# The down product of a SwiGLU layer in the seven-product form, over even and odd chunks

## The chip, the cores and the metric

One core of one Trainium2 chip runs the whole program in one launch. The metric is the device time in microseconds (us) of one execution; before the change it is 2521.99 us (median of 3 runs, 2521.57 to 2523.63).

## The reference, cut to what matters

One layer of a streaming encoder over 560 tokens (16 meta, 512 prompt, 32 sample). All data is fp32, D_MODEL = 2048, D_FF = 5632.

```python
xn = rms_norm(h, g_pre_mix); proj = xn @ w_in           # 2048 x 6144
attn = stick-breaking attention, 8 heads; conv = gated short conv, 8 groups
h = h + rms_norm(mix @ w_out, g_post_mix)               # 2048 x 2048
xf = rms_norm(h, g_pre_ffn)
ff = silu(xf @ w_gate) * (xf @ w_up)                    # 2048 x 5632, twice
h = h + rms_norm(ff @ w_down, g_post_ffn)               # 5632 x 2048
```

The feed-forward part needs only the 544 tokens after the meta tokens (TL = 544, in two halves of TH = 272).

## The kernel before

Activations lie transposed: a chunk is 128 features on the partitions, tokens in the free dimension. Every matmul takes a 128x128 block of weights and 272 (or 280) tokens. Each fp32 product is made of three fp32r matmuls: rounded weights times rounded activations, rounded weights times the rest of the activations, rest of the weights times rounded activations. So every tile of weights (128 x 1024 values) is read by a DMA, rounded by ScalarE (`copy` into `t_hi`) and its rest taken by VectorE (`tile_rest`, `tensor_tensor` subtract into `t_lo`). Both live in a ring of RING_T = 4 tiles; ScalarE may round tile i only when the product of tile i - 4 is done (`tile_high`, L1313).

The stages in order of time: input transposed and normalised; heads and conv groups (loops over pairs, partly `Fori` hardware loops on each engine); out product; norm; gate and up products; down product; last norm, transposes and stores.

**Gate and up.** They use a seven-product form of a 2x2 block product (Strassen-Winograd): the 16 input chunks are split into halves A11..A22 (chunk halves 0 to 7 and 8 to 15, by token halves), and each step (44 of them; even ones gate, odd ones up) makes two output chunks from two panels of weights (8 chunks x 256 columns, 1 MB each). Seven tiles B11, B21, T2, T3, T1, T4, B22 (T1 to T4 are combinations that VectorE makes with `combine`, L1708) give seven products of 8 x 3 = 24 matmuls (`product`, L955). The combinations of the activations, `xs`, are made once. Products accumulate in three PSUM banks of a step in the order "acababa"; what is needed from a bank in between is copied out by ScalarE (`m1`, `u2`, `m7`) or added by VectorE (`c11`, `c22`, `c21`). The last product of a step, B22, waits for `c22_made` (the wait stands ahead of `product` for q == B22).

**SwiGLU.** In each even step VectorE multiplies the pair's values into `hid` (2 chunks x 544), ScalarE rounds them (`round_hidden`, L1352), VectorE takes the rest (`hidden_rest`, L1786), and SyncE stores both to DRAM (L573, L574).

**Down.** The plain form: 44 chunks of hidden values times 16 output chunks, in 4 blocks of 12, 12, 12 and 8 chunks. For each block and each pair of output chunks a tile of 4 chunks x 256 columns (`down_raw`, 6 buffers, L595) is loaded, split and multiplied with both token halves of the block's hidden values (`ffs`, loaded from DRAM for a whole block, L600): 48 matmuls per tile (L1004). The sums stay in PSUM over a block, then VectorE copies or adds 128 x 544 values to `y` (L1851, L1855). The hidden values of the next-but-one block are loaded when a block has ended. In the last block ScalarE squares finished chunks, GpSimd adds the squares, and two pairs of matmuls (L716) sum them over partitions for the last norm.

**Queues.** All loads and stores named here are issued by SyncE (SP) in one written order, each behind its waits, and are served in turn. Each other engine too runs its instructions in the order written.

Of the kernel before, what the change touches and what calls it, by code (L numbers as in the profile page):

```python
# [20 lines left out]
F32 = mybir.dt.float32  # L21
# [8 lines left out]
def build_layer(nc, x_prompt, x_sample, cache_k, cache_v, state_conv, meta, w_in, w_out, conv_w,  # L30
# [85 lines left out]
    with ExitStack() as ctx:  # L116
# [34 lines left out]
        def carve(at, n):  # L151
# [34 lines left out]
        gate = sb_at("gate", 189440, [P, 2, TL])  # L186
        hid = sb_at("hid", 193792, [P, 2, TL])
        hid_hi = sb_at("hid_hi", 198144, [P, 2, TL], F32R)
        hid_lo = sb_at("hid_lo", 202496, [P, 2, TL], F32R)
        ffs = sb_at("ffs", 0, [P, 2, max(SUBS), 2, SUB, TL], F32R)  # L190
        down_raw = [sb_at(f"down_raw{j}", at + h * 4096, [P, SUB, 2 * P])
                    for j, (at, h) in enumerate((at, h) for at in (181248, 121856, 173056) for h in range(2))]
        y_parts = [sb_at("y_left", 104448, [P, KH, TL]), sb_at("y_right", 189440, [P, KH, TL])]
        h2_back = sb_at("h2_back", 0, [P, KC, TL])
        y_tok = sb_at("y_tok", 34816, [P, 4, QB + 1, P])
        y_sq = [sb_at(f"y_sq{j}", 45056 + j * TL * 4, [P, TL]) for j in range(2)]
        y_sq_sum = sb_at("y_sq_sum", 45056 + 2 * TL * 4, [P, TL])
# [4 lines left out]
        ff_hi_scr = nc.dram_tensor("ff_hi_scr", (P, FF, TL), F32, kind="Internal").ap()  # L202
        ff_lo_scr = nc.dram_tensor("ff_lo_scr", (P, FF, TL), F32, kind="Internal").ap()
# [133 lines left out]
        hid_made = sem("hid_made")  # L337
        hid_rounded = sem("hid_rounded")
# [3 lines left out]
        down_loaded = [sem(f"down_loaded{j}") for j in range(6)]  # L342
        ffs_loaded = [[sem(f"ffs_loaded{j}_{k}") for k in range(3)] for j in range(2)]
        down_left = sem("down_left")
# [88 lines left out]
        w_down_v = w_down[0].rearrange("(k p) n -> p k n", p=P)  # L433
# [3 lines left out]
        DOWN0 = 7 * STEPS  # L437

        down_tiles = [(b, m, u) for b in range(len(SUBS)) for m in range(KC // 2) for u in range(SUBS[b])]
        first_chunk = [SUB * sum(SUBS[:b]) for b in range(len(SUBS))]  # L440
        first_tile = [KC // 2 * sum(SUBS[:b]) for b in range(len(SUBS))]

# [9 lines left out]

        def block_of_weights(step, half, n):
            return panel_of(step, half)[0][:, :, n * P:(n + 1) * P]

        def raw_tile(i):

            step, q = i // 7, i % 7
            if q == T2:
                return t2_raw[:, :, :]  # L460
            half, n = {B11: (0, 0), T1: (0, 0), T3: (0, 1), B21: (1, 0), T4: (1, 0), B22: (1, 1)}[q]
            return block_of_weights(step, half, n)

        def tile_of(ring, i):
            return ring[:, i % RING_T, :].rearrange("p (k n) -> p k n", n=P)
# [4 lines left out]
        def quarter(buf, t, n):  # L470
            return buf[:, n, t * TH:(t + 1) * TH]

        def down_tile_of(ring, i):
            return ring[:, i % RING_T, :].rearrange("p (k n) -> p k n", n=2 * P)
# [5 lines left out]
        def _(sp):  # L480
# [53 lines left out]
            with sp.Fori(0, HEADS // 2 - 1) as r:  # L534
                load_pair(r + 1, HEAD_COLS)
            with sp.Fori(HEADS // 2, (HEADS + GROUPS) // 2) as p:
                load_pair(p, CONV_COLS)
# [16 lines left out]
            with sp.Fori(2, KC // 2) as q:  # L554
                load_out(q)

            def load_panel(step, half):
                tile, loaded, _ = panel_of(step, half)
                src = gate_up[step % 2][:, KH * half:KH * (half + 1), step // 2 * 2 * P:(step // 2 + 1) * 2 * P]
                sp.dma_start(tile[:, :, :], src).then_inc(loaded, 16)  # L560
# [10 lines left out]
            def store_hidden(j):  # L571
                sp.wait_ge(hid_split, j + 1)
                sp.dma_start(ff_hi_scr[:, 2 * j:2 * j + 2, :], hid_hi[:, :, :].bitcast(F32)).then_inc(hid_stored, 16)  # L573
                sp.dma_start(ff_lo_scr[:, 2 * j:2 * j + 2, :], hid_lo[:, :, :].bitcast(F32)).then_inc(hid_stored, 16)  # L574

            for step in range(1, STEPS):
# [6 lines left out]
                if step > 3 and step % 2 == 0:  # L583
                    store_hidden(step // 2 - 2)
                load_panel(step, 0)
# [17 lines left out]
            for d in range(6):
                if d % 2 == 0:
                    sp.wait_ge(tile_lo, (7 * (LAST - 1) + 7, 7 * LAST + T1 + 1, 7 * LAST + 7)[d // 2])
                load_down(d)
                if d % 2:
                    continue
                sp.wait_ge(product_done, 7 * LAST + d // 2 + 1)
                if d == 0:  # L610
                    sp.wait_ge(hid_stored, 32 * (FF // 2 - 1))
                load_hidden(0, d // 2)
            for u in range(3):
                sp.wait_ge(product_done, 7 * LAST + 4 + u)
                load_hidden(1, u)
            store_hidden(FF // 2 - 1)
            for d in range(6, len(down_tiles)):
                b, m, u = down_tiles[d]
                if m == 1 and u == 0 and b in (1, 2):
                    sp.wait_ge(product_done, DOWN0 + first_tile[b])  # L620
                    sp.wait_ge(hid_stored, 32 * (FF // 2))
                    for v in range(SUBS[b + 1]):
                        load_hidden(b + 1, v)
                if m == 1 and u == 0 and b == 3:
                    sp.wait_ge(product_done, DOWN0 + first_tile[b])
                    sp.dma_start(h2_back[:, :, :], h_scr[:, :, LATE]).then_inc(h2_back_loaded, 16)
                sp.wait_ge(tile_lo, DOWN0 + d - 6 + 1)
                load_down(d)
# [15 lines left out]
        def _(pe):  # L644
# [245 lines left out]
            with pe.Fori(1, HEADS // 2) as p:  # L890
# [4 lines left out]
            with pe.Fori(HEADS // 2 + 1, (HEADS + GROUPS) // 2) as p:  # L895
# [35 lines left out]
            with pe.Fori(1, KC // 2) as q:  # L931
# [52 lines left out]
            for d, (b, m, u) in enumerate(down_tiles):  # L984
                i = DOWN0 + d
                pair = b * KC // 2 + m
                pe.wait_ge(tile_lo, i + 1)
                if m == 0:
# [991 lines left out]
```

## Time and profile before

| | us |
|---|---|
| median of 3 runs | 2521.99 |
| the profiled execution | 2524.61 |
| its span, first to last instruction | 2522.9 |
| TensorE matmul busy (18716 matmuls) | 2440.0 (97%) |
| VectorE busy | 1252.4 (50%) |
| ScalarE busy | 915.5 (36%) |
| granted TensorE clock, mean | 0.981 |

The page's chain of work that ended last lies 90% on TensorE: 36% on L955 (gate and up), 30% on L422 (input and out products), 19% on L1004 (down). A matmul's listed duration (about 290 ns) overlaps its neighbours'; the distance between two is what counts.

### The profile page before, as it was taken

Reading aid. Unit: us, or ns where it says so; the run is one execution under the profiler, and the core shown is the slowest. Engines: PE = TensorE matmul, PEld = TensorE weight load, DVE = VectorE, ACT = ScalarE, POOL = GpSimd, SP = SyncE. Lnnn points to the kernel's source line nnn. Section 1 sums busy time; section 2 is a strip of 40 time slices with the busy share of each in tenths; the row PEclk is TensorE's granted clock in tenths of the full one; section 3 lists DMA queues with packets and bytes.
Section 4 is the critical chain, followed back from the end, with each engine's and each line's share of the span. In section 5 each row is a group of like instructions: output and inputs, shape, how many; then the busy total and the mean of one; then the engine's idle time right before and its main releaser. Section 6 shows DMA issues by size and latency. Waiting matters only on the chain.

```text
span 2522.9 us, 43292 instructions
## 1 busy us (share of the span) xinstructions
PE 2440.0 (97%) x18716; PEld 2394.1 (95%) x18716; DVE 1252.4 (50%) x1387; ACT 915.5 (36%) x1177; POOL 99.0 (4%) x155
## 2 busy tenths in 40 slices
PE   8999999999999985999999999999999999999997
PEld 7999999999999984999999999999999999999996
DVE  5324332444353228777777767676765222222144
ACT  6344444422342224444444444444443111111123
POOL 0000000000011100000000000000000000000024
PEclk9999999999999996999999999999999999999997
DMA  7223222232225321434343434333336516242222
GB/s 235 83 64 89 80 80 65 85 92 84 80 70 167 89 75 64 134 119 136 118 137 118 137 118 136 119 131 124 126 129 262 187 43 232 76 171 85 105 93 71
DMA packets 313049, 290.66 MB, mean 115 GB/s; under 512 B 8348, under 2 KB 296500, under 8 KB 309956
## 3 DMA queue, kind: packets, MB, share of 16 engines
q1 hardware_dynamic: 298528, 281.70, 34.5%
q10 hardware_dynamic: 14372, 6.77, 0.9%
q8 instruction: 118, 1.93, 0.3%
q14 instruction: 31, 0.25, 0.0%
HBM read 245.82 MB, written 42.61 MB: 114 GB/s over the span
## 4 chain that ended last, share of the span: by engine, by line
PE 90%; DVE 5%; DMA 2%; ACT 2%; SPq 1%; issue 1%; POOL 0%; POOLq 0%; ACTq 0%; DVEq 0%
PE ps L955 36%; PE ps L422 30%; PE ps L1004 19%; PE ps L722 4%; DMA down_raw<-in_w_down_dram 2%; DVE xs L1716 1%; PE ps L666 1%; DMA misc<-in_x_sample_dram 0%; DVE misc L1720 0%; DVE y_left L1880 0%; DVE wide L1685 0%; DVE misc L1689 0%; DVE y_right L1880 0%; ACT xs L1320 0%; DVE t_lo L1695 0%
## 5 line engine op out<-in xcount | busy, mean ns | idle before, releaser
L955 PE MATMUL ps<-xs,t_hi 128*128 128x272 f32 x4928 | 940.5, 291 | 33.1 <-DVE xs L1716 19.1
L955 PEld LDWEIGHTS ps<-xs,t_hi 128*128 128x128 f32 x4928 | 780.9, 190 | 34.7 <-issue 32.2
L955 PE MATMUL ps<-xs,t_lo 128*128 128x272 f32 x2464 | 716.6, 291 | 0.0
L1004 PE MATMUL ps<-ffs,t_hi 128*128 128x272 f32 x2816 | 470.7, 290 | 12.7 <-DVE y_right L1855 7.3
L955 PEld LDWEIGHTS ps<-xs,t_lo 128*128 128x128 f32 x2464 | 467.3, 190 | 0.0
L1695 DVE TENSOR_TENSOR t_lo<-panel,t_hi 128x1024 fp32r<-128x1024 f32 x261 | 319.4, 1224 | 255.7 <-ACT t_hi L1313 255.7
L422 PE MATMUL ps<-act_hi,w_hi 128*128 128x272 f32 (+1 forms) x2048 | 435.4, 294 | 3.5 <-DVE act_lo L1532 2.3
L422 PE MATMUL ps<-act_lo,w_hi 128*128 128x272 f32 (+1 forms) x2048 | 427.0, 290 | 0.0
L422 PE MATMUL ps<-act_hi,w_lo 128*128 128x272 f32 (+1 forms) x2048 | 426.8, 290 | 0.0
L1004 PEld LDWEIGHTS ps<-ffs,t_hi 128*128 128x128 f32 x2816 | 402.2, 190 | 13.4 <-issue 7.5
L1313 ACT CAST t_hi<-panel 128x1024 fp32r<-128x1024 f32 x261 | 272.8, 1045 | 191.8 <-PE ps L955 185.4
L422 PEld LDWEIGHTS ps<-act_hi,w_hi 128*128 128x128 f32 x2048 | 322.8, 189 | 7.5 <-DVE act_lo L1532 3.0
L422 PEld LDWEIGHTS ps<-act_hi,w_lo 128*128 128x128 f32 x2048 | 324.2, 189 | 0.0
L422 PEld LDWEIGHTS ps<-act_lo,w_hi 128*128 128x128 f32 x2048 | 323.8, 189 | 0.0
L1004 PE MATMUL ps<-ffs,t_lo 128*128 128x272 f32 x1408 | 293.3, 290 | 0.0
L1791 DVE TENSOR_TENSOR t_lo<-down_raw,t_hi 128x1024 fp32r<-128x1024 f32 x88 | 109.8, 1248 | 304.1 <-ACT t_hi L1358 304.1
L408 DVE TENSOR_TENSOR w_lo<-w_raw,w_hi 128x1024 fp32r<-128x1024 f32 x126 | 157.9, 1254 | 192.2 <-ACT w_hi L402 190.7
L1358 ACT CAST t_hi<-down_raw 128x1024 fp32r<-128x1024 f32 x88 | 92.2, 1048 | 403.2 <-PE ps L1004 305.8
L402 ACT CAST w_hi<-w_raw 128x1024 fp32r<-128x1024 f32 x128 | 133.7, 1046 | 282.8 <-PE ps L422 222.1
L1004 PEld LDWEIGHTS ps<-ffs,t_lo 128*128 128x128 f32 x1408 | 221.7, 190 | 0.0
L1346 ACT ACTIVATE m<-ps 128x272 f32<-128x272 f32 x88 | 34.9, 397 | 150.1 <-PE ps L955 150.1
L1313 ACT CAST t_hi<-t_raw 128x1024 fp32r<-128x1024 f32 x44 | 46.2, 1049 | 69.3 <-PE ps L955 69.3
(174 smaller groups left out, 1547.1 us busy)
## 6 DMA issues: line engine op xcount, KB each, us to landing
w_raw<-in_w_in_dram SPq DMA_DIRECT2D x96, 512.0 KB, 3.8
panel<-in_w_up_dram SPq DMA_DIRECT2D x44, 1024.0 KB, 5.1
down_raw<-in_w_down_dram SPq DMA_DIRECT2D x88, 512.0 KB, 5.2
panel<-in_w_gate_dram SPq DMA_DIRECT2D x43, 1024.0 KB, 6.4
w_raw<-in_w_out_dram SPq DMA_DIRECT2D x32, 512.0 KB, 3.9
ff_hi_scr<-hid_hi SPq DMA_DIRECT2D x22, 544.0 KB, 2.7
ff_lo_scr<-hid_lo SPq DMA_DIRECT2D x22, 544.0 KB, 4.4
ffs<-ff_hi_scr SPq DMA_DIRECT2D x11, 1088.0 KB, 11.7
```

The source lines that it names most:

```text
L402: nc.scalar.copy(w_hi[:, k % SLOTS, :], raw_slot(k)).then_inc(hi_ready, 1)
L408: engine.tensor_tensor(w_lo[:, k % SLOTS, :], raw_slot(k), w_hi[:, k % SLOTS, :].bitcast(F32), ALU.subtract).then_inc(lo_ready, 1)
L422: mm = nc.tensor.matmul(out[:, h, :], w[:, k, col:col + width], x[:, x_at + k, token + h * half:token + (h + 1) * half], start=begins, sto ...
L666: return nc.tensor.transpose(out, src, ident[0:n, 0:n])
L722: return nc.tensor.matmul(out, w, x, start=start, stop=True, skip_group_check=True)
L955: mm = nc.tensor.matmul(out, w[:, k, :], xs[:, x, part, k, :], start=begins and k == 0 and w is hi and part == 0, stop=k == KH - 1 and w i ...
L1004: mm = nc.tensor.matmul(ps[:, 4 * (pair % 2) + 2 * n + h, 0:TH], w[:, k, n * P:(n + 1) * P], ffs[:, b % 2, u, part, k, h * TH:(h + 1) * TH ...
L1313: nc.scalar.copy(tile_of(t_hi, i), raw_tile(i)).then_inc(tile_hi, 1)
L1346: A(out[:, :], step_bank(step, letter), ACT.Copy).then_inc(made, 1)
L1358: nc.scalar.copy(down_tile_of(t_hi, i), down_raw[d % 6][:, :, :]).then_inc(tile_hi, 1)
L1695: V.tensor_tensor(tile_of(t_lo, i), raw_tile(i), tile_of(t_hi, i).bitcast(F32), ALU.subtract) .then_inc(tile_lo, 1)
L1791: V.tensor_tensor(down_tile_of(t_lo, i), down_raw[d % 6][:, :, :], down_tile_of(t_hi, i).bitcast(F32), ALU.subtract).then_inc(tile_lo, 1)
```

## The change

The down product gets the same seven-product form as gate and up. The 44 hidden chunks are taken as 22 pairs (even chunk, odd chunk): they are the two halves of the inner dimension. They come in six blocks of 4, 4, 4, 4, 3, 3 pairs (KBS). Each of 24 down steps (4 per block, NQ) makes four output chunks from two panels (even, odd) of KBS x 512 columns. A tile is KBS chunks x 256 columns, and a product is KBS x 2 x 3 matmuls of 272 tokens. The seven combinations of the hidden values are made per pair by VectorE (`hidden_sums`, 4 operations of 272 values), rounded, split and stored in DRAM (7 x 272 values per pair and part, before 4 x 272), and loaded per product of a block into a ring `xd` of 12 slots. `hid_lo` now lies over `hid`, so the next up step's first write to `hid` waits for the stores. After each of the seven products VectorE copies or adds 128 x 2 x 272 values from PSUM to `y`, and TensorE waits for that before it goes on in the same banks. All `Fori` loops are written out as Python loops. The rest stays. In the order of work, `round_hidden` moves from behind the tile T4+1 to behind the `m7` copy, `hidden_rest` moves to the next (odd) step, and the panel of half 0 is now loaded ahead of the stores.

```diff
+    KBS = [4, 4, 4, 4, 3, 3]
+    NQ = KC // 4
+    DSTEPS = NQ * len(KBS)
+    XD = 12
+        hid = sb_at("hid", 193792, [P, 7, TH])
+        hid_lo = sb_at("hid_lo", 193792, [P, 7, TH], F32R)
+        hid_hi = sb_at("hid_hi", 201408, [P, 7, TH], F32R)
+        xd = sb_at("xd", 0, [P, XD, 2, max(KBS), TH], F32R)
...
+        def down_banks(d, q):
+            pair = {"a": 3 * (d % 2), "c": 1, "b": 2}["acababa"[q]]
+            return ps[:, 2 * pair:2 * pair + 2, 0:TH]
... SyncE
+            def load_hidden(i):
+                b, q = i // 7, i % 7
+                sp.wait_ge(hid_stored, 32 * first_pair[b + 1])
+                for part in range(2):
+                    sp.dma_start(xd[:, i % XD, part, 0:KBS[b], :].bitcast(F32),
+                                 ff_scr[part][:, HID_OF[q], first_pair[b]:first_pair[b + 1], :])\
+                      .then_inc(xd_loaded[i % XD], 16)
+            def load_hidden_after(step, q):
+                if step == LAST and q < 6:
+                    sp.wait_ge(product_done, 7 * step + q + 1)
+                    load_hidden(2 * q)
+                    load_hidden(2 * q + 1)
+                elif step >= STEPS and (step - STEPS) % NQ == NQ - 1:
+                    i = (step - STEPS) // NQ * 7 + q + XD
+                    if i < 7 * len(KBS):
+                        sp.wait_ge(product_done, 7 * step + q + 1)
+                        load_hidden(i)
+            for step in range(1, ALL):
...
+                load_panel(step, 0)
+                if step >= LAST + 2:
+                    for q in range(4, 7):
+                        load_hidden_after(step - 2, q)
+                if step > 3 and step % 2 == 0 and step // 2 - 2 < FF // 2:
                     store_hidden(step // 2 - 2)
-                load_panel(step, 0)
+                if step >= LAST + 1:
+                    for q in range(2):
+                        load_hidden_after(step - 1, q)
...
                     sp.wait_ge(tile_lo, 7 * (step - 1) + T1 + 1)
                 load_panel(step, 1)
+                if step >= LAST + 1:
+                    for q in range(2, 4):
+                        load_hidden_after(step - 1, q)
... TensorE
+            for d in range(DSTEPS):
+                b, m = d // NQ, d % NQ
+                for q in range(7):
...
+                    in_y = {B11: 7 * (d - 1), B21: 7 * (d - 1) + 2, T2: 7 * d + 1, T3: 7 * (d - 1) + 6,
+                            T1: 7 * d + 3, T4: 7 * d + 4, B22: 7 * d + 5}[q]
+                    if in_y > 0:
+                        pe.wait_ge(y_added, in_y)
+                    for n in range(2):
+                        for k in range(KBS[b]):
+                            for w, part in ((hi, 0), (hi, 1), (lo, 0)):
+                                mm = nc.tensor.matmul(out[:, n, :], w[:, k, n * P:(n + 1) * P], xd[:, slot, part, k, :],
... ScalarE, gate and up steps
             def round_hidden(j):
-                act.wait_ge(hid_made, j + 1)
+                act.wait_ge(hid_summed, 4 * (j + 1))
...
-                if is_gate and step:
-                    round_hidden(j - 1)
...
                 copy_out(m7, step, T3, "b", m7_copied, c22_made)
+                if is_gate and step:
+                    round_hidden(j - 1)
                 tile_high(ahead)
... VectorE
+            def hidden_sums(j):
+                d21, d11, d12, d22, s1, s2, s4 = (hid[:, h, :] for h in range(7))
+                dve.wait_ge(hid_made, j + 1)
+                V.tensor_tensor(s1, d21, d22, ALU.add).then_inc(hid_summed, 1)
+                dve.wait_ge(hid_summed, 4 * j + 1)
+                V.tensor_tensor(d21, d11, d21, ALU.subtract).then_inc(hid_summed, 1)
+                V.tensor_tensor(s2, s1, d11, ALU.subtract).then_inc(hid_summed, 1)
+                dve.wait_ge(hid_summed, 4 * j + 3)
+                V.tensor_tensor(s4, d12, s2, ALU.subtract).then_inc(hid_summed, 1)
... down steps: the order per step
+                if d:
+                    take_down(d - 1, B22)
+                tile_rest(7 * step + 3)
+                combine(step, T4)
+                if d == 0:
+                    times_gate(LAST)
+                if d == 1:
+                    hidden_rest(FF // 2 - 1)
+                take_down(d, B11)
+                tile_rest(7 * step + 4)
...
+                take_down(d, B21)
+                tile_rest(7 * step + 5)
+                take_down(d, T2)
+                tile_rest(7 * step + 6)
...
+                take_down(d, T3)
+                tile_rest(ahead); combine(step + 1, T1)
+                take_down(d, T1)
+                combine(step + 1, T2); tile_rest(ahead + 1)
+                take_down(d, T4)
+                combine(step + 1, T3); tile_rest(ahead + 2)
... every engine: `with x.Fori(a, b) as p:` becomes `for p in range(a, b):`
```

## Rows read from the trace of the kernel before

**Rows 1.** By stretch: length, busy us of PE PEld DVE ACT POOL, clock, DMA share, GB/s
```profile
50.00:935.00 885.00, 881.64 (x6705) 856.61 (x6706) 315.82 (x419) 318.65 (x381) 54.04 (x119) 1.00 0.30 88
1022.00:1938.00 916.00, 915.86 (x7250) 915.89 (x7251) 656.52 (x689) 404.94 (x542) 0.00 (x0) 1.00 0.39 131
...
2082.00:2106.00 24.00, 18.66 (x148) 18.44 (x147) 2.08 (x3) 2.09 (x2) 0.00 (x0) 0.96 0.97 370
2106.00:2235.00 129.00, 129.00 (x1013) 129.00 (x1013) 38.95 (x39) 23.07 (x22) 0.00 (x0) 0.98 0.26 82
...
2253.00:2380.00 127.00, 127.00 (x1015) 127.00 (x1015) 36.81 (x36) 22.05 (x22) 0.00 (x0) 1.00 0.25 79
2380.00:2399.00 19.00, 11.73 (x92) 11.54 (x92) 2.98 (x4) 3.13 (x3) 0.00 (x0) 0.88 1.01 359
2399.00:2486.00 87.00, 87.00 (x673) 86.85 (x673) 28.20 (x29) 22.24 (x29) 19.59 (x15) 0.97 0.19 58
```

**Rows 2.** Chain that ended last, pieces by start: start us, us, what
```profile
1937.94 144.34 PE ps L1004 x1152
...
2398.65 87.14 PE ps L1004 x672
```

**Rows 3.** ScalarE's timeline of an even step and the next: start us, us, operation
```profile
1432.52 0.40 ACT L1346 ACTIVATE m<-ps 128x272 f32<-128x272 f32 x1 [1.98 <-PE ps L955]
...
1441.60 0.40 ACT L1346 ACTIVATE m<-ps 128x272 f32<-128x272 f32 x1 [1.69 <-PE ps L955]
...
1444.63 1.05 ACT L1313 CAST t_hi<-panel 128x1024 fp32r<-128x1024 f32 x1 [1.69 <-PE ps L955]
...
1447.66 1.05 ACT L1313 CAST t_hi<-t_raw 128x1024 fp32r<-128x1024 f32 x1 [1.32 <-PE ps L955]
...
1453.71 0.40 ACT L1346 ACTIVATE m<-ps 128x272 f32<-128x272 f32 x1 [1.69 <-PE ps L955]
```

**Rows 4.** VectorE's timeline of the same even step
```profile
1439.94 1.23 DVE L1695 TENSOR_TENSOR t_lo<-panel,t_hi 128x1024 fp32r<-128x1024 f32 x1 [1.73 <-ACT t_hi L1313]
1441.09 1.28 DVE L1786 TENSOR_TENSOR hid_lo<-hid,hid_hi 128x1088 fp32r<-128x1088 f32 x1
...
1445.25 0.43 DVE L1764 TENSOR_TENSOR gate<-ps,m 128x272 f32<-128x272 f32 x1
1445.60 1.22 DVE L1708 TENSOR_TENSOR t_raw<-panel,panel 128x1024 f32<-128x1024 f32 x1
```

**Rows 5.** Groups of instructions, shapes kept apart: count | busy us, mean ns | idle before
```profile
L1695 DVE TENSOR_TENSOR t_lo<-panel,t_hi 128x1024 fp32r<-128x1024 f32 x261 | 319.4, 1224 | 255.7 <-ACT t_hi L1313 255.7
...
L1352 ACT CAST hid_hi<-hid 128x1088 fp32r<-128x1088 f32 x22 | 24.1, 1097 | 3.4 <-DVE hid L1780 3.4
...
L1855 DVE TENSOR_TENSOR y_left<-ps,y_left 128x544 f32<-128x544 f32 x24 | 17.1, 722 | 26.8 <-PE ps L1004 26.8
...
L1716 DVE TENSOR_TENSOR xs<-misc,xs 128x2176 fp32r<-128x2176 f32 x6 | 14.4, 2422 | 3.9 <-ACT xs L1320 3.9
...
L1320 ACT CAST xs<-misc 128x2176 fp32r<-128x2176 f32 x6 | 11.9, 2004 | 20.6 <-DVE misc L1746 9.0 <-DVE misc L1720 6.9 <-DVE t_lo L1695 4.7
```

**Rows 6.** Busy time by stretch, where hidden values are loaded around 1938 us
```profile
1922.00:1938.00 16.00, 16.00 (x129) 16.00 (x128) 7.79 (x10) 5.82 (x7) 0.00 (x0) 1.00 1.04 400
1944.00:1960.00 16.00, 16.00 (x130) 16.00 (x129) 5.10 (x5) 2.09 (x2) 0.00 (x0) 1.00 1.02 420
```

**Rows 7.** DMA issues: count, KB each, median us from issue to landing
```profile
panel<-in_w_up_dram SPq DMA_DIRECT2D x44, 1024.0 KB, 5.1
```

**Rows 8.** The end of the last block: ScalarE, VectorE, GpSimd timelines
```profile
2484.25 1.28 ACT L1068 ACT_TABLE_LOAD   x1
...
2488.51 0.71 ACT L1057 ACTIVATE rstd<-ps,eps 128x544 f32<-128x544 f32 x1 [1.27 <-PE ps L716]
...
2485.82 0.72 DVE L1855 TENSOR_TENSOR y_right<-ps,y_right 128x544 f32<-128x544 f32 x1 [2.28 <-PE ps L1004]
...
2484.31 1.35 POOL L1893 TENSOR_TENSOR y_sq_sum<-y_sq_sum,y_sq 128x544 f32<-128x544 f32 x1 [7.67 <-ACT y_sq L1122]
```

More of the change, by code:

```diff
@@ L889, in _ @@
                 head(0, u, u, u > 0, False)
-            with pe.Fori(1, HEADS // 2) as p:
+            for p in range(1, HEADS // 2):
                 for u in range(2):
@@ L894, in _ @@
                 group(HEADS // 2, u, HEADS + u, first_pair=True)
[L895 removed]
+            for p in range(HEADS // 2 + 1, (HEADS + GROUPS) // 2):
                 for u in range(2):
@@ L930, in _ @@
             two_chunks(T_OUT, mix_chunk, 2, {6: last_norm_and_rows})
-            with pe.Fori(1, KC // 2) as q:
+            for q in range(1, KC // 2):
                 for c in range(2):
@@ L1246, in _ @@
                 head(0, u, u, u > 0, False)
-            with act.Fori(1, HEADS // 2) as p:
+            for p in range(1, HEADS // 2):
                 for u in range(2):
@@ L1294, in _ @@
             out_round(0, 2)
-            with act.Fori(1, KC // 2 - 1) as q:
+            for q in range(1, KC // 2 - 1):
                 out_round(q, 0)
@@ L1635, in _ @@
                 head(0, u, u, u > 0, False)
-            with dve.Fori(1, HEADS // 2) as p:
+            for p in range(1, HEADS // 2):
                 for u in range(2):
@@ L1673, in _ @@
             out_round(0, 2)
-            with dve.Fori(1, KC // 2 - 1) as q:
+            for q in range(1, KC // 2 - 1):
                 out_round(q, 0)
@@ L1802, in _ @@
                     x_rest(S3, 6, a21)
+                if step % 2 and step > 1:
+                    hidden_rest(step // 2 - 1)
                 tile_rest(7 * step + 4)
@@ L1818, in _ @@
                     c11(step)
+                if step % 2:
+                    c11(step)
                 if after_up:
-                    hidden_rest(step // 2 - 1)
-                if step < LAST:
+                    hidden_sums(step // 2 - 1)
+                tile_rest(ahead)
+                combine(step + 1, T1)
+                c22(step)
+                combine(step + 1, T2)
+                tile_rest(ahead + 1)
+                c21(step)
+                combine(step + 1, T3)
+                tile_rest(ahead + 2)
@@ L1925, in mask @@
                 last.then_inc(ready, 1)
-            with pool.Fori(1, HEADS + 1) as heads:
+            for heads in range(1, HEADS + 1):
                 mask(relu, sp_made, sp_ready, heads)
```

309 lines of the change are left out of this document (126 added, 183 removed).

## The prediction, made before the changed kernel ran

> **What bounds the kernel now.** I read the busy table by stretch first. From 1022 to 1938 us (gate and up) TensorE is busy 915.86 of 916 us, VectorE 656.5 and ScalarE 404.9; from 50 to 935 us TensorE is busy 881.6 of 885; in the down stage the same holds except near the block boundaries [rows 1]. So the count of matmuls times the distance between two sets the time, and an engine off the path matters only if it comes later than TensorE needs it. The timeline gives that distance: the m copy of a step is released by its first product, and it comes again after 21.19 us (1432.52 to 1453.71) [rows 3]. A step has 168 matmuls, so 126.1 ns each and 3.03 us per product of 24. The down stage runs at 144.34 / 1152 = 125.3 ns [rows 2], so the plain form is not slower per matmul. Third, the chain: down begins at 1937.94 and its last piece ends at 2398.65 + 87.14 = 2485.79 [rows 2], 547.85 us for 4224 matmuls (44 x 16 x 2 x 3). At 125.3 ns they would take 529.3; the rest is stalls at two boundaries (5.3 us in 2082 to 2106, 7.3 us in 2380 to 2399) and a granted clock of 0.98 and 0.97 behind them [rows 1].
>
> **Change, part one: fewer matmuls.** New count: 22 pairs x 4 groups x 7 products x 2 x 3 = 3696. Each has its own weights, as in gate and up, so I take that distance: 3696 x 126.1 ns = 466.1 us. Removed: 547.85 - 466.1 = **-81.7 us**. This contains the old boundary stalls; new ones are added below.
>
> **Part two: gate and up steps get more vector work.** VectorE has slack on average: 656.5 of 916, or 15.2 per step of 21.2. The change adds per pair of steps four operations of 272 (0.35 each back to back, from 1445.25 to 1445.60 [rows 4]), and the split grows from 1088 to 1904 values. What counts is the order in the even step. Taking the times of rows 3 and 4: VectorE is free of the B22 tile's rest at 1441.09. There the four sums now stand; two of them wait for the one just ahead (0.08 each, the difference of 0.43 and 0.35), so the last ends at 1441.09 + 3 x 0.35 + 0.43 + 0.16 = 1442.73. Rounding 1904 values lies between 1.10 (1088) and 2.00 (2176) [rows 5], by size 1.78: ScalarE, which did it earlier in the step, now does it at 1442.8 to 1444.55, ahead of the next step's B11 tile. That cast, which could begin after 1441.9 before, ends at 1445.55; VectorE's rest of it takes 1.15 (1439.94 to 1441.09), `combine` T1 another 1.13, and `c22` behind them runs from 1447.83 to 1448.26; before it began at 1445.25 [rows 4]. TensorE is done with T4 at 1447.66 as the release at L1313 shows [rows 3], some 0.2 after its last issue, so it wants B22, and `c22_made` with it, at 1447.45. It stands 0.8 us. The odd step has room to catch up, so this comes once in each of the 21 even steps that carry a pair: **+17 us**. Bounds: 0 if the sums and the rounding come out 0.8 shorter together; 1.4 us per even step (29 us) if each sum costs its full 0.43 and the rounding 2.0.
> The odd step: `hidden_rest` takes about 2.05 (1.28 for 1088 [rows 4], 2.42 for 2176 [rows 5]), the stores of 1.95 MB need 4.9 us at 0.40 MB/us [rows 6] and about 2 to land, so they are down some 13 us into the step, and `c11`, which now waits for them, has been ready at 11.4. Behind `c11` lie about 8.2 us of VectorE work; it ends near 22, when the next step's first tile can be split anyhow. Nothing; its cover is VectorE's idle time before tiles, 255.7 us over the stage or 5.8 per step [rows 5]. Without it each us here would be 21.
>
> **Part three: the entry into the down stage.** In step 43, SP must move in this order: the stores of pair 20 (1.95 MB), four slots of hidden values (each 2 x 0.557 MB, 4.46 in all), the odd panel of step 44 (1.05), four slots and a panel (5.5), four slots and a panel (5.5). Around 1938 the queue moved 400 to 420 GB/s in loads of this kind [rows 6]; I take 0.40 MB/us. Zero is the first product of step 43. The stores can start at 6.2 (split behind the T4 combination). 7.46 MB later it is 24.9, and with some 2 us to land (1.05 MB take 5.1 [rows 7] against 2.6 by rate) the panel is there at 26.8. T2 is combined and B21 split by 29.2 (two operations of 1.14). TensorE wants B21 at 21.2 + 3.0 = 24.2: 5.0 us. Then T2 needs y to have taken B11's result, and that stands in VectorE's line behind c21, T3, two tiles, T4 and `times_gate` (5.9 us), where TensorE has only B21's 3.03 to cover it: 2.9. One more us falls before B22. The next 11 MB bring step 45's odd panel at 54.3; its B21 is split at 56.7 and wanted at 54.2: 2.5; then the same line, now with the 2.05 us split of the last pair in it: 5.5. Together **+17 us**. At 0.33 it is 27, at 0.30 37. I take 0.40 because rows 6 show this mix.
> In sentences of their own: the Trainium skill, DMA: Bandwidth & Descriptors, Specifications, puts HBM at about 358 GB/s per core. The trace goes above it, 400 and 420 GB/s [rows 6], though other boundaries show 359 and 370 [rows 1]. By that rule the two panels come later, the entry costs 22 instead of 17, and the kernel ends near 2485.
>
> **Part four: the steady down steps.** A step of 4 pairs gives VectorE 7 rests and 4 combinations of 1024 (1.14) and 7 results of 544 (0.72 listed, 0.64 back to back [rows 5]): 12.5 + 4.5 = 17.0 us of 21.2. A step of 3 pairs: tiles of 768 at about 0.87, 9.6 + 4.5 = 14.1 of 15.9, or 88%. It fits, and a result has one product's time (3.03 or 2.27) before TensorE wants its bank. Later boundaries load 7 slots over seven products (7.8 MB in 21 us), the panel needed early has 3.3 MB ahead of and with it: it lands 14 us into the step and is wanted at 24. No term; bounds 0 to the rival below. The weights' bytes stay 46 MB.
>
> **Part five: small terms.** Clock behind the entry's stalls: 2399 to 2486 ran 673 matmuls at 129.3 ns and clock 0.97 after a stall of 7.3, against 125.1 at 1.00 [rows 1]: 2.8; I take **+3**. End: the last result now carries chunks 14 and 15 together. Before, result to `Ln` was 2485.82 to 2488.51; now 0.72 + 0.66 + a table load of 1.28 and its 0.2 [rows 8] + 0.66, two row sums, or GpSimd's chain of 1.35 adds: about 5.4 in place of 2.7, **+2.7**. `Fori` written out: TensorE's whole idle time from 50 to 935 is 3.4 us [rows 1], so at most -3.4; the written-out gate and up stage has no gaps, so I see no loss. 0.
>
> **Sum.** From the profiled execution's 2524.61 (its span of 2522.9 and 1.7 around it): -81.7 + 17 + 17 + 3 + 2.7 = -42, which gives 2482.6. The median of the runs is 2.6 lower, so **2480 us**.
>
> **Rivals.** A, it goes better: the sums and the rounding are 0.8 us quicker in the even step and the entry is half as dear. For it: both are differences of small numbers (0.8 of 21). Against: the entry's bytes are fixed. 2480 - 17 - 9 = 2454.
> B, the queue is slower, for stores now run in pieces of 1088 bytes and before in 4352. At 0.30 MB/us the entry costs 37 and each later boundary 2: 2480 + 21 = about 2501. For it: a slice at a boundary showed 359 GB/s; against: weights arrive in 1024-byte pieces already.
> C, it gets slower: TensorE and VectorE fall into lockstep in the down steps. VectorE waits in line for each result and each cast, seven times a step each, and idle time there is lost. It can afford 21.2 - 17.0 = 4.2 us idle (1.8 in the short steps). In gate and up it idles 5.8 per step for casts; takes before idled 26.8/24 = 1.1 each, 7.8 for seven [rows 5]. With half of both, 6.8: 16 x 2.6 + 8 x 5.0 = 81 us more, 2561. It decides against the change from 6 us idle per step. Against it: idle time before a cast is VectorE being early, and it shrinks as work is added.
>
> **Chances and range.** Forecast 0.66, with its own range 2466 to 2495; A 0.12, B 0.13, C 0.09. The range goes to A's and B's values with little beyond: 2458 to 2505. A measurement here can tell about 0.2% (5 us). Faster by more: all of forecast, A and B, and a little of C, 0.90; within: 0.03; slower: 0.07.
>
> **What would show it.** 3696 matmuls at 126 ns; one TensorE wait of 0.8 us per even step for `gate<-ps,m` of L1764; waits of 5, 3, 2.5 and 5.5 us for a tile's rest and for y in the first two down steps, and almost none after; VectorE busy near 80% there. Wrong, if the first down steps run on without a stall, if waits for y come in every step, or if the distance in down is not 126.

## The result, and the profile after

The changed kernel takes 2493.64 us (median of 4 runs, 2491.42 to 2494.7) against 2522.81 for the kernel before on the same chip (4 runs). The ratio is 0.9882, 95% interval 0.9865 to 0.9899: it is 29 us faster. Forecast were 2480 and a gain of 42. The profiled execution took 2493.23 us, its span 2491.5.

First the busy time by stretch (columns as in [rows 1]).

```profile
50.00:935.00 885.00, 881.88 (x6707) 856.84 (x6705) 316.34 (x418) 318.83 (x380) 54.05 (x119) 1.00 0.30 88
...
1016.00:1960.00 944.00, 924.76 (x7265) 919.99 (x7266) 709.82 (x775) 425.75 (x542) 0.00 (x0) 1.00 0.44 143
1960.00:1966.00 6.00, 4.13 (x33) 3.91 (x31) 0.00 (x0) 0.00 (x0) 0.00 (x0) 1.00 1.01 390
1966.00:2007.00 41.00, 26.83 (x193) 26.03 (x193) 30.39 (x35) 14.04 (x13) 0.00 (x0) 0.90 0.78 305
2007.00:2050.00 43.00, 43.00 (x323) 43.00 (x324) 34.84 (x37) 13.66 (x13) 0.00 (x0) 0.94 0.48 145
2050.00:2100.00 50.00, 50.00 (x399) 50.00 (x398) 40.36 (x41) 16.82 (x16) 0.00 (x0) 1.00 0.73 261
...
2350.00:2400.00 50.00, 50.00 (x400) 50.00 (x399) 46.10 (x58) 18.40 (x22) 0.00 (x0) 1.00 0.48 163
```

The reader is to see three things against [rows 1]. The front has not moved. TensorE is no longer full in gate and up (924.8 of 944). In the down stage it is full from 2007 to 2400, with VectorE busy 81 to 92% of the time; most of the loss there sits in the first 46 us. The list of who TensorE waited for names the places (columns: total us, times, longest).

```profile
PE ps L975 <- DVE gate L1784: 18.1, 21, 0.9
...
PE ps L1032 <- DVE t_lo L1711: 8.6, 2, 7.0
...
PE ps L1032 <- DVE y_left L1874: 6.6, 2, 5.3
PE ps L736 <- POOL y_sq_sum L1938: 3.6, 1, 3.6
PE ps L1032 <- DVE y_left L1876: 1.1, 2, 0.9
...
PE ps L1032 <- DVE y_right L1876: 0.5, 1, 0.5
```

L975 is the gate and up product, L1784 `c22`, L1711 `tile_rest`, L1032 the down product, L1874 and L1876 its results into y. With the first and last down matmul (1937.8 to 2485.5 before, 1960.9 to 2449.3 after) and the first m copy of gate and up (1016.35 before, 1015.85 after) the span divides so:

| stretch | before | after | change | forecast |
|---|---|---|---|---|
| up to the first m copy | 1016.35 | 1015.85 | -0.5 | 0 |
| from there to the first down matmul | 921.45 | 945.05 | +23.6 | +17 |
| down matmuls | 547.7 | 488.4 | -59.3 | -61.7 |
| last of them to the end of the span | 37.4 | 42.2 | +4.8 | +2.7 |
| span | 2522.9 | 2491.5 | -31.4 | -42 |

The even step, which answers to [rows 3] and [rows 4], first ScalarE, then VectorE, then TensorE's first matmuls of B22:

```profile
1755.91 0.40 ACT L1369 ACTIVATE m<-ps 128x272 f32<-128x272 f32 x1 [1.69 <-PE ps L975]
1757.17 1.79 ACT L1375 CAST hid_hi<-hid 128x1904 fp32r<-128x1904 f32 x1 [0.86 <-DVE hid L1811]
1758.86 1.99 ACT L1336 CAST t_hi<-panel 128x1024 fp32r<-128x1024 f32 x2
```

```profile
1756.69 0.44 DVE L1811 TENSOR_TENSOR hid<-hid 128x272 f32<-128x272 f32 x1
1759.93 1.23 DVE L1711 TENSOR_TENSOR t_lo<-panel,t_hi 128x1024 fp32r<-128x1024 f32 x1 [2.80 <-ACT t_hi L1336]
1761.07 1.22 DVE L1725 TENSOR_TENSOR panel<-panel 128x1024 f32<-128x1024 f32 x1
1762.21 0.43 DVE L1784 TENSOR_TENSOR gate<-ps,m 128x272 f32<-128x272 f32 x1
```

```profile
1762.79 0.48 PE L975 MATMUL ps<-xs,t_hi 128*128 128x272 f32 x2 [0.86 <-DVE gate L1784]
```

The chain is the forecast one: sums, rounding of 1.79 us, cast, rest, combination, `c22`, which ends 6.73 us after the m7 copy began (6.66 forecast). TensorE's next matmul starts 0.15 later.

The entry into the down stage, VectorE's timeline:

```profile
1956.61 0.43 DVE L1784 TENSOR_TENSOR hid<-ps,m 128x272 f32<-128x272 f32 x1
1968.72 1.23 DVE L1725 TENSOR_TENSOR t_raw<-panel,panel 128x1024 f32<-128x1024 f32 x1 [11.68 <-DMA panel<-in_w_down_dram]
...
1995.90 1.22 DVE L1725 TENSOR_TENSOR t_raw<-panel,panel 128x1024 f32<-128x1024 f32 x1 [5.62 <-DMA panel<-in_w_down_dram]
...
2003.98 2.13 DVE L1815 TENSOR_TENSOR hid_lo<-hid,hid_hi 128x1904 fp32r<-128x1904 f32 x1
2006.04 0.72 DVE L1874 COPY y_left<-ps 128x544 f32<-128x544 f32 x1
```

Twice VectorE stands before the odd panel, 11.68 and 5.62 us. Step 43 began about 1939.7 (the wait's end at 1936.66 and one product of 3.03), so VectorE goes on 29.0 and 56.2 us into it; forecast were 26.8 and 54.3.

### The profile page after: what moved, and what is told of

Its sections match the earlier page's. It is cut to its first block, busy times and chain, and to the rows that moved or that the text cites. A ratio compares the mean times of both kernels' runs of the same rounds, so it can differ in the third digit from the quotient of the medians.

```text
span 2491.5 us, 42064 instructions
## 1 busy us (share of the span) xinstructions
PE 2382.3 (96%) x18188; PEld 2329.9 (94%) x18188; DVE 1553.6 (62%) x1755; ACT 1009.2 (41%) x1257; POOL 103.7 (4%) x155
## 4 chain that ended last, share of the span: by engine, by line
PE 80%; DVE 10%; issue 4%; ACT 4%; DMA 2%; SPq 1%; POOL 0%; POOLq 0%; ACTq 0%; DVEq 0%
PE ps L427 30%; PE ps L975 28%; PE ps L1032 17%; PE ps L742 4%; ACT t_hi L1336 2%; DVE t_lo L1711 2%; DVE panel L1725 2%; SPq L606 1%; DMA panel<-in_w_down_dram 1%; DMA ff_lo_scr<-hid_lo 1%; PE ps L686 1%; DVE xs L1733 1%; DVE misc L1737 0%; DVE y_left L1925 0%; DVE wide L1701 0%
## 5 line engine op out<-in xcount | busy, mean ns | idle before, releaser
L975 PE MATMUL ps<-xs,t_hi 128*128 128x272 f32 x4928 | 943.3, 291 | 51.0 <-DVE xs L1733 19.1
L975 PEld LDWEIGHTS ps<-xs,t_hi 128*128 128x128 f32 x4928 | 780.7, 190 | 57.2 <-issue 54.7
L975 PE MATMUL ps<-xs,t_lo 128*128 128x272 f32 x2464 | 716.6, 291 | 0.0
L1711 DVE TENSOR_TENSOR t_lo<-panel,t_hi 128x1024 fp32r<-128x1024 f32 (+1 forms) x405 | 485.9, 1200 | 195.1 <-ACT t_hi L1336 187.2
L1336 ACT CAST t_hi<-panel 128x1024 fp32r<-128x1024 f32 (+1 forms) x405 | 411.9, 1022 | 470.5 <-PE ps L1032 230.6
L1032 PE MATMUL ps<-xd,t_hi 128*128 128x272 f32 x2464 | 470.3, 290 | 16.9 <-DVE t_lo L1711 8.6
L975 PEld LDWEIGHTS ps<-xs,t_lo 128*128 128x128 f32 x2464 | 467.3, 190 | 0.0
L1032 PEld LDWEIGHTS ps<-xd,t_hi 128*128 128x128 f32 x2464 | 390.4, 190 | 18.7 <-issue 9.6
L1032 PE MATMUL ps<-xd,t_lo 128*128 128x272 f32 x1232 | 358.1, 291 | 0.0
L1032 PEld LDWEIGHTS ps<-xd,t_lo 128*128 128x128 f32 x1232 | 233.5, 190 | 0.0
L1336 ACT CAST t_hi<-t_raw 128x1024 fp32r<-128x1024 f32 (+1 forms) x68 | 69.8, 1026 | 64.1 <-PE ps L1032 35.7
L1725 DVE TENSOR_TENSOR t_raw<-panel,panel 128x1024 f32<-128x1024 f32 (+1 forms) x67 | 79.4, 1185 | 22.2 <-DMA panel<-in_w_down_dram 17.3
L1482 DVE TENSOR_TENSOR misc<-misc 128x1440 f32<-128x1440 f32 x8 | 13.3, 1658 | 114.3 <-ACT misc L1119 114.3
```

The lines of the kernel that those rows point to most:

```text
L975: mm = nc.tensor.matmul(out, w[:, k, :], xs[:, x, part, k, :], start=begins and k == 0 and w is hi and part == 0, stop=k == KH - 1 and w i ...
L1032: mm = nc.tensor.matmul(out[:, n, :], w[:, k, n * P:(n + 1) * P], xd[:, slot, part, k, :], start=q in (B11, B21, T3) and k == 0 and w is h ...
L1336: nc.scalar.copy(tile_of(t_hi, i), raw_tile(i)).then_inc(tile_hi, 1)
L1711: V.tensor_tensor(tile_of(t_lo, i), raw_tile(i), tile_of(t_hi, i).bitcast(F32), ALU.subtract)\
L1725: V.tensor_tensor(out, x, y, ALU.subtract).then_inc(t_made, 1)
```

## The experiments

The theory: the 81.7 us of matmuls are really gone, and three orders of work take some 45 of them back (by the gains expected below): the rounding's place on ScalarE, the panels' place in SyncE's queue, and GpSimd's adds at the end. Rivals: VectorE's added work itself, the bytes themselves, and the lockstep of rival C. The experiments ran on several chips, on which the kernel before had medians of 2520.9 to 2523.3 us; so a distance to the changed kernel, which ran on another occasion, is uncertain by some 2 us.

### e1_round_later

```diff
-                if is_gate and step:
-                    round_hidden(j - 1)
                 tile_high(ahead)
+                if is_gate and step:
+                    round_hidden(j - 1)
                 tile_high(ahead + 1)
```

> Changed kernel with one move on ScalarE: in even gate steps the rounding of the pair (hid_hi<-hid, 1.79 us) stands behind the cast of the next step's B11 tile, not ahead of it. Theory (the order costs the gate and up stage 23 us): the 21 waits of TensorE for gate<-ps,m vanish, the pair of steps takes 42.4 us and not 43.5, and the whole about 2470 us, 22 to 24 below the changed kernel. Rival (VectorE's added work, four sums and a split of 1904 values, does it, wherever the rounding stands): waits stay, the time stays within 5 us of 2493.

Measured: 2469.73 us (2468.25 to 2472.0), ratio 0.9791 (0.9775 to 0.9807); 24 us below the changed kernel. The 21 waits for `gate<-ps,m` are gone from the list; of L975's waits for L1784 one of 0.4 us stays. Its ScalarE, then VectorE in an even step:

```profile
1737.39 0.40 ACT L1369 ACTIVATE m<-ps 128x272 f32<-128x272 f32 x1 [1.69 <-PE ps L975]
1737.68 1.04 ACT L1336 CAST t_hi<-panel 128x1024 fp32r<-128x1024 f32 x1
1738.64 1.79 ACT L1375 CAST hid_hi<-hid 128x1904 fp32r<-128x1904 f32 x1
```

```profile
1738.17 0.44 DVE L1811 TENSOR_TENSOR hid<-hid 128x272 f32<-128x272 f32 x1
1738.76 1.23 DVE L1711 TENSOR_TENSOR t_lo<-panel,t_hi 128x1024 fp32r<-128x1024 f32 x1
1739.90 1.22 DVE L1725 TENSOR_TENSOR panel<-panel 128x1024 f32<-128x1024 f32 x1
1741.04 0.44 DVE L1784 TENSOR_TENSOR gate<-ps,m 128x272 f32<-128x272 f32 x1
```

With the same vector work, `c22` begins 3.65 us after the m7 copy and not 6.30. The stretch from the first m copy to the first down matmul is 921.9 us (1014.98 to 1936.9), 0.5 from before. The order did all of it; the rival falls. The 21 waits of 0.86 us (18.1) had cost 23.1: in the changed kernel B22 of two even steps begins at 1762.79 and at 1806.26, 43.47 us apart, against 2 x 21.19 without a wait. The gap is longer than the listed idle time because that is counted from the listed end of the last matmul, 0.29 us after its start, where the next one would have started 0.126 after it: 0.16 us more. The first two matmuls behind the wait then take 0.32 us and not 0.25.

### e2_entry_order

```diff
+                if step == LAST + 1:
+                    sp.wait_ge(tile_lo, 7 * (step - 1))
+                    load_panel(step, 0)
+                    store_hidden(step // 2 - 2)
+                    sp.wait_ge(tile_lo, 7 * (step - 1) + T1 + 1)
+                    load_panel(step, 1)
+                    slots_after(0, 0, 2)
+                    slots_after(1, 2, 4)
+                    continue
+                if step == LAST + 2:
+                    sp.wait_ge(tile_lo, 7 * (step - 1))
+                    load_panel(step, 0)
+                    slots_after(2, 4, 6)
+                    slots_after(3, 6, 7)
+                    sp.wait_ge(tile_lo, 7 * (step - 1) + T1 + 1)
+                    load_panel(step, 1)
+                    slots_after(5, 7, XD)
+                    continue
```

> Changed kernel with another order on SyncE in steps 43 and 44 alone: the odd panel of down step 0 ahead of the first slots, the even panel of down step 1 ahead of slots 4 to 6, and slots 7 to 11 behind the odd panel of down step 1. Bytes are the same. Theory (the panels' place in the queue makes the entry stall): the waits of 7.0, 1.3, 0.9, 1.6 and about 5 us in the first two down steps go to under 2 in all, and the time falls by 15 to 20 us to about 2476. Rival (the bytes themselves, 13 MB in 40 us, make it): the stall moves to the slots' own arrival and the time falls by less than 6 us.

Measured: 2479.95 us (2477.95 to 2483.43), ratio 0.9831 (0.9815 to 0.9848), 13.7 below the changed kernel; 15 to 20 were expected, and waits of under 2 us in all, so a miss in size. Its waits of TensorE in the down stage:

```profile
PE ps L1055 <- DVE y_left L1897: 3.7, 1, 3.7
...
PE ps L1055 <- issue: 1.2, 1, 1.2
PE ps L1055 <- DVE t_lo L1734: 0.6, 1, 0.6
PE ps L1055 <- DVE y_right L1899: 0.5, 1, 0.5
...
PE ps L1055 <- DVE y_left L1899: 0.2, 1, 0.2
```

The wait of 7.0 is 0.6. The sum falls from 16.8 to 6.2, and the down matmuls take 474.1 us instead of 488.4 (1961.7 to 2435.8). Of these 14.3 us the waits make 10.6; the rest goes mostly with the clock, for from 2007 to 2050 TensorE now starts 343 matmuls at a granted clock of 1.00, and in the changed kernel 323 at 0.94. Of the waits that are left, 3.7 is for y's first result in down step 1, which VectorE takes behind the split of the last pair. The 1.2 listed as issue stands before the fifth product of down step 0. Its slot of hidden values now comes behind a panel: its second part is issued at 1961.18, such a load lands 14.0 us later in the median, and the product starts at 1975.19. That much of the rival, a stall that moves to the slots, is there.

### e3_tail_on_pe

```diff
+            parts = [(y_sq_added, KC - 4, y_sq_sum[:, :]), (y_squared, KC - 3, y_sq[0][:, :]),
+                     (y_squared, KC - 2, y_sq[1][:, :]), (y_squared, KC - 1, y_sq_last[0][:, :]),
+                     (y_squared, KC, y_sq_last[1][:, :])]
...
-                    if c == KC - 1:
+                    if c == KC - 2:
                         load_log_table(3)
...
-            for c in range(KC - 1):
+            for c in range(KC - 4):
                 add_square(pool, y_sq_sum[:, :], y_sq[c % 2][:, :], y_squared, y_sq_added, c)
```

> Changed kernel with another end: GpSimd adds only the squares of chunks 0 to 11, TensorE sums those of 12 to 15 over partitions itself (10 matmuls for 4), and the table load stands ahead of the square of chunk 14. Theory (the end waits for three adds of 1.35 us in line on GpSimd behind the last result): last matmul of down to Ln falls from 9.9 us to about 3.6, time 2487 to 2488. Rival (the adds have cover and TensorE's slow small matmuls decide): no gain or up to 2 us more.

Measured: 2491.62 us (2489.52 to 2492.9), 2 below the changed kernel, where 6 were expected; with four runs each a difference of 2 us is at the edge of what can be told. The 9.9 us in my expectation was misread: it starts from the result before the last. From the last result to `Ln` the changed kernel takes 7.6 us, before took 2.7 [rows 8]. The changed kernel's end, ScalarE, GpSimd and VectorE, and the busy time of the stretch in which TensorE sums over partitions (columns as in [rows 1]):

```profile
2457.20 0.71 ACT L1080 ACTIVATE rstd<-ps,eps 128x544 f32<-128x544 f32 x1 [4.13 <-PE ps L736]
```

```profile
2448.83 4.29 POOL L1938 TENSOR_TENSOR y_sq_sum<-y_sq_sum,y_sq 128x544 f32<-128x544 f32 x3 [3.21 <-ACT y_sq L1145]
```

```profile
2449.59 0.72 DVE L1876 TENSOR_TENSOR y_right<-ps,y_right 128x544 f32<-128x544 f32 x1 [1.53 <-PE ps L1032]
```

```profile
2453.00:2457.20 4.20, 4.00 (x8) 2.53 (x8) 0.00 (x0) 0.07 (x1) 0.12 (x1) 0.50 0.00 0
```

Three adds in line, then four matmuls (eight records). TensorE has stood 3.61 us before them, and the granted clock is 0.50, the level of 1.2 GHz: they take 4.0 us, where the kernel before needed 1.18 twice at a clock of 1.00. In the experiment TensorE starts at once and keeps the clock (1.00 from 2448.6 to 2453.4), but its ten fp32 matmuls are now the line:

```profile
2448.62 1.08 PE L1046 MATMUL ps<-y_sq_sum,neg 128*128 128x272 f32 x4
2449.54 3.83 PE L1046 MATMUL ps<-y_sq,neg 128*128 128x272 f32 x16
```

The last down matmul to the end of the span is 39.3 us instead of 42.2 (2448.5 to 2487.8), a gain of 2.9. From the last down matmul to `Ln` it is 4.9 us instead of 7.9; 3.6 were expected.

### e4_before_unrolled

The edit to the kernel before: every `with x.Fori(a, b) as p:` becomes `for p in range(a, b):`.

> Kernel before with all Fori loops written out and nothing else. Theory (loops cost TensorE nothing, its queue is never empty at their ends): within 2 us of before; TensorE idle from 50 to 935 us stays near 3.4. Rival (loop ends cost register and branch time, or fetching more code costs): 3 us faster or some us slower.

Measured: ratio 1.0003 (0.9994 to 1.0012) over 11 and 15 runs, and TensorE is busy 881.88 of 885 us from 50 to 935 (881.64 before). Written-out loops are worth nothing here, either way.

### e5_no_pool_adds

```diff
-            for c in range(KC - 1):
-                add_square(pool, y_sq_sum[:, :], y_sq[c % 2][:, :], y_squared, y_sq_added, c)
...
-            row_sums(y_sq_added, y_squared, y_sq_sum[:, :], y_sq[(KC - 1) % 2][:, :])
+            pe.wait_ge(y_squared, KC)
+            for h, bank in enumerate((bank_a, bank_b)):
+                mm = nc.tensor.matmul(bank[:, 0:LHALF], neg1[:, :], y_sq[(KC - 1) % 2][:, h * LHALF:(h + 1) * LHALF],
+                                      start=True, stop=True)
```

> Changed kernel that leaves out GpSimd's adds of the squares in the last down block and sums over partitions the last square alone, so the last norm is not the reference's. Theory (VectorE's operations of 0.95 us that take up to 2.1 us in the last block are slowed by GpSimd's adds beside them): no such operation is over 1.0 us, the small waits for y in the last block vanish, and with the end's adds gone the time is about 2484. Rival (they are slowed by the DMA or by ScalarE's squares): they stay at up to 2.1 us.

The kernel leaves out GpSimd's adds, the waits of ScalarE's squares for them, and the sums over all squares but the last. Measured: 2488.63 us (2488.27 to 2489.75), 5 below the changed kernel; 9 were expected. From 2385 to 2450 us, VectorE's rests and first combinations in the changed kernel, then in this one (count | busy, mean ns | idle):

```profile
L1711 DVE TENSOR_TENSOR t_lo<-panel,t_hi 128x768 fp32r<-128x768 f32 x22 | 24.5, 1113 | 0.9
L1725 DVE TENSOR_TENSOR panel<-panel 128x768 f32<-128x768 f32 x3 | 5.2, 1731 | 0.0
```

```profile
L1717 DVE TENSOR_TENSOR t_lo<-panel,t_hi 128x768 fp32r<-128x768 f32 x22 | 21.0, 955 | 1.6
L1731 DVE TENSOR_TENSOR panel<-panel 128x768 f32<-128x768 f32 x3 | 2.9, 952 | 0.0
```

So it is GpSimd's adds that lengthen them; the rival falls, for the loads and ScalarE's squares are still there. The waits for `y_right` are gone, the down matmuls take 486.4 us instead of 488.4, and the end 39.5 instead of 42.2. Results read from PSUM (128 x 544) did not change: 716 to 722 ns with and without.

The end holds something that the theory of e3 did not see:

```profile
2450.80 1.37 PE L1040 MATMUL ps<-y_sq,neg 128*128 128x272 f32 x4 [3.56 <-ACT y_sq L1417]
```

Without any add, TensorE still waits 3.56 us (3.61 in the changed kernel), now for ScalarE, whose square of chunk 15 stands behind the table load. In the changed kernel that square ends at 2453.07 and the last add at 2453.12. The two lines are equally long, so taking the adds away alone shortens no wait; the 2.7 us come from the two matmuls fewer and a granted clock of 0.81 instead of 0.50.

### e6_more_vector_work

```diff
+            def tile_rest_twice(i):
+                dve.wait_ge(tile_hi, i + 1)
+                V.tensor_tensor(tile_of(t_lo, i), raw_tile(i), tile_of(t_hi, i).bitcast(F32), ALU.subtract)\
+                    .then_inc(again, 1)
+                dve.wait_ge(again, 2 * (i // 7 - STEPS) + i % 7 - 3)
+                tile_rest(i)
...
                 take_down(d, B11)
-                tile_rest(7 * step + 4)
+                tile_rest_twice(7 * step + 4)
...
                 take_down(d, B21)
-                tile_rest(7 * step + 5)
+                tile_rest_twice(7 * step + 5)
```

> Changed kernel in which VectorE takes the rests of the T1 and T4 tiles of each down step twice (2.4 us more per step of 4 pairs, 1.9 per step of 3). Theory (a step has 21.2 - 17.0 = 4.2 us of slack, the short ones 1.8, and waits in line only turn slack into idle time): the 16 long steps stay at 21.2 us, the 8 short ones grow by 0 to 1 us, time 2493 to 2502. Rival (VectorE and TensorE in lockstep, each us of vector work is on the path): 24 steps x 2.2, about 2546.

Measured: 2504.36 us (2502.69 to 2508.16), 10.7 above the changed kernel, 2 above what I expected and 42 below the rival's. Of some 54 us of added vector work, a fifth comes through. TensorE's waits in down:

```profile
PE ps L1033 <- DVE y_right L1884: 7.1, 2, 4.2
PE ps L1033 <- DVE t_lo L1712: 6.8, 1, 6.8
PE ps L1033 <- DVE y_left L1882: 6.8, 4, 4.8
...
PE ps L1033 <- DVE y_left L1884: 2.8, 3, 1.9
```

From 2030 to 2400 there is not one wait, though VectorE is busy 232.9 of 250 us from 2050 to 2300 (207.9 in the changed kernel) and TensorE starts the same 1985 matmuls; the new ones stand in the last block, where steps are short and GpSimd adds beside VectorE. There is no lockstep, and the steady steps have over 2 us of slack.

### e7_all_three

The edit: e1, e2 and e3 together.

> The three moves together. If they are independent the time is 2493.6 - 23 - 17 - 6, about 2448 us. If VectorE, at some 80% in the down steps, only hid behind the stalls, part of them comes back as waits for y and the time stays over 2455.

Measured: 2455.6 us (2455.53 to 2457.69), ratio 0.9736 (0.9719 to 0.9752), 38 below the changed kernel. The single gains were 23.9, 13.7 and 2.0, 39.6 in all: the three are independent to within 2 us. The expected 2448 was the sum of expected gains, not of the measured ones. The time lies 0.6 us over the 2455 that I had set as the bound for a hidden VectorE; the bound was badly placed, for the waits list shows no wait for VectorE in the steady steps. The down matmuls take 475.0 us, the waits of e2 are the same.

### e8_all_and_last_pair, and e9_all_three_again

```diff
-                    if d == 0 and q == 6:
+                    if d == 0 and q == 8:
                         round_hidden(FF // 2 - 1)
...
-                if d == 1:
-                    hidden_rest(FF // 2 - 1)
                 take_down(d, B11)
...
+                if d == 1:
+                    hidden_rest(FF // 2 - 1)
                 take_down(d, T2)
```

> The three moves together, and the last pair's rounding and split moved too: ScalarE rounds it behind the cast of down step 1's B21 tile, VectorE splits it behind the rest of the T1 tile of down step 1, ahead of the result of T2. Theory (the wait of 3.7 us that is left in the second down step is the split of 2.05 us, and the 2.2 us that VectorE stands behind the rounding, ahead of the result that TensorE wants): that wait goes, total waits in the first two down steps fall from 5.5 to about 1.5 us, time 2451 to 2452. Rival (it is the odd panel's arrival): the wait stays and the time stays at 2455 to 2456.

> The three moves together once more, beside the one above on the same chip, so that a difference of 4 us can be told: 2455 to 2456.

Measured: e8 2456.89 us (2455.03 to 2458.47), ratio 0.9747 (0.9733 to 0.976); e9, the kernel of e7 again, 2454.52 (2452.43 to 2457.42), ratio 0.9736 (0.9723 to 0.9749). No gain: a miss. The trace of e8 shows the wait of 3.7 us shrink to 1.6, and new ones behind it in down step 2:

```profile
1969.40 0.48 PE L1056 MATMUL ps<-xd,t_hi 128*128 128x272 f32 x2 [1.63 <-DVE y_left L1910]
...
1988.65 0.51 PE L1056 MATMUL ps<-xd,t_hi 128*128 128x272 f32 x2 [0.85 <-DVE t_lo L1747]
1995.17 0.79 PE L1056 MATMUL ps<-xd,t_hi 128*128 128x272 f32 x2 [3.24 <-DVE y_right L1910]
```

VectorE can combine T2 of that step, for which it needs the odd panel, at 1986.22 in e8 (5.63 us idle before it) and at 1985.42 in e7 (0.50 idle):

```profile
1986.22 1.22 DVE L1761 TENSOR_TENSOR t_raw<-panel,panel 128x1024 f32<-128x1024 f32 x1 [5.63 <-DMA panel<-in_w_down_dram]
```

```profile
1985.42 1.23 DVE L1761 TENSOR_TENSOR t_raw<-panel,panel 128x1024 f32<-128x1024 f32 x1 [0.50 <-DMA panel<-in_w_down_dram]
```

Counted from the first down matmul (1938.80 in e8, 1939.62 in e7) that is 47.4 us and 45.8: the panel comes 1.6 us later, and in e9, where that matmul starts at 1941.39, it is 45.9 again. SyncE's own rows, e8 and then e7, say why:

```profile
1974.23 0.52 SPq L600 DMA_DIRECT2D ff_hi_scr<-hid_hi  x1
```

```profile
1971.44 0.52 SPq L600 DMA_DIRECT2D ff_hi_scr<-hid_hi  x1
```

The store of the last pair waits for its split, and in SyncE's written order it stands ahead of that odd panel. The split was moved back, so the store is issued 35.4 us into the stage and not 31.8, and the panel behind it at 36.7 and not 33.6. So the theory of the 3.7 us wait holds, but what was won at it is lost at the panel: the waits of the first three down steps are 7.6 us in all instead of 5.5. The trace points at an order again and not at the bytes alone; the kernel with e8's move and this panel ahead of the store was not run. The best version is e7's, 2.6% below before and 1.5% below the changed kernel.

## Why the prediction was right or wrong

**Direction and mechanism were right; the gain came out at 29 instead of 42.** By the profiled executions it is 31.4 against 42. The range of 2458 to 2505 holds the 2493.6. The 10.6 us that are missing lie in the gate and up stage (6.6), the down matmuls (2.4) and the end (2.1), less 0.5 ahead of them.

**Part one, fewer matmuls.** Right. The distance of the seven-product form holds: 399 to 400 matmuls per 50 us in the steady stretch, 125 to 126 ns each, and 3696 records where 4224 were. The down matmuls take 488.4 us: 466.1, listed waits of 16.8, and 5.5 for the clock (part five) and for the 0.16 us by which each of the seven waits loses more than its listed idle time.

**Part two, gate and up, is where 6.6 of the 10.6 us went.** The chain was right to 0.07 us, and that it comes 21 times; e1 shows cause and cure. Mis-sized was what one such wait costs: 1.10 us, not 0.8. TensorE's want was placed right: its last matmul before the wait starts at 1761.64, so the next was due 5.86 us after the m7 copy began (5.85 forecast). But `c22` was 0.07 later than reckoned, and I left out the 0.15 us from its end to the first matmul and the 0.07 that the first two matmuls lose. So 23.1 us where 17 stood. The odd step was right: `c11` stands 2.8 us on average (50.3 us in 18 waits from 1100 to 1900, 39.9 of them in 15 waits that end with the stores; 1.6 were reckoned), and TensorE hardly notices (0.8 us in four waits).

**Part three, the entry.** 16.9 forecast (17 in the sum), 16.0 measured in the first two down steps, 16.8 in the whole stage; e2 shows that their place in the queue made most of it. That the sum came out so well is in part luck, for single waits were off: 7.0, 1.3, 0.9, 1.6, 5.3 where I had 5.0, 2.9, 1.0, 2.5, 5.5. The first panel came 2.2 us later than reckoned, and what it delayed first was then shorter. The queue moved 343 GB/s from 1947 to 1952, while the stores ran, 378 to 1960 and 390 to 1966, and 396 over 1952 to 1984. So 0.40 MB/us was near for the loads and too high for the start; the second panel was still only 1.9 us late. By the 358 that the Trainium skill gives (DMA: Bandwidth & Descriptors, Specifications) the entry would have cost 22; the trace goes above that figure.

**Part four, steady steps.** Right: no wait from 2007 to 2400, and e6 bears the slack out. Not foreseen was GpSimd's hand in the last block: 2.0 us in the down matmuls by e5.

**Part five.** Clock: 323 matmuls in 43 us at 0.94 and 193 in 26.83 at 0.90, against 126.1 ns, cost 2.3 and 2.5 us, 4.8 where 3 stood (some 0.7 of it belongs to the waits, by the 0.16 us each). A mean of 0.90 or 0.94 means that part of the stretch ran at 1.2 GHz and the rest at 2.4: behind the wait of 7.0 us the granted clock is 0.50 from 1971.14 to 1974.50, and behind that of 5.3 us 0.50 from 2006.90 to 2010.50; behind the 1.6 us it is 1.00. The end: +4.8 instead of +2.7. I had set GpSimd's adds beside the table load as an either-or and taken 5.4 us from result to `Ln`; it was 7.6. Until TensorE could begin it was 3.6 us, on both lines alike; then the four matmuls took 4.0 at a granted clock of 0.50, and some 1.9 were reckoned. The step that failed here is that I gave them the time of the kernel before, in which TensorE stood only 0.39 us among them and the clock was 1.00. `Fori`: 0, shown by e4.

**Rivals.** A did not come by itself (e1 and e2 made it happen). B did not: later boundaries cost nothing. C did not come, and e6 refutes it. B's price was also added up too low: the entry at 37 instead of 17 and 2 us at each of five later boundaries make 30 and not 21; nothing hangs on it.

## What to carry to other kernels

When a busy engine gets a new long operation, the question is not its share but which short operation stands behind it in line and who waits for that: a rounding of 1.8 us, 21 times, cost 23 to 24 us, and moving it by one instruction gave them back. At a change of stage, look at the queue's order byte by byte: what is needed first goes first, and loads for later blocks go last. The same question holds for the cure: in e8 the operation that was moved back also released a store, and a panel stood behind the store. And a wait of some microseconds costs its length and, where the clock falls, the slow matmuls behind it.

## What the runs showed of the hardware that was not expected

VectorE's SBUF-to-SBUF operations slow down while GpSimd adds: 128x768 from 955 ns to a mean of 1113 over 22 and at most 1954 (the median stays at 949, so only those beside an add are longer), a combination to 1731 on average over three; GpSimd's own adds of 128x544 went from 1.35 us to a mean of 1695 ns over 12 there. VectorE's operations that read PSUM were not slowed. The three longest VectorE operations that have an add beside them (1.95, 2.12 and 2.12 us, from 2405.74, 2411.16 and 2428.01) each end 0.81 to 0.83 us after GpSimd's row does. That looks like an operation that stands until the add is over and then takes its own time, rather than two that share; it is inferred from these rows alone.

The listed idle time of a wait is not what the wait costs: 0.86 us of idle lengthened the pair of steps by 1.09, of which 0.16 is the way in which idle time is counted and 0.07 the first two matmuls behind it.

At the end of the down stage the same four matmuls take 2.4 us in the kernel before and 4.0 in the changed one, with a granted clock of 1.00 and 0.50; TensorE had stood 3.61 us before the slow ones.
